# FFN phases of a transformer trunk: 512-wide matmul passes split into 256-wide ones behind a few wide passes

## The reference

```python
D_MODEL = 1024
SEQ = 256
D_FF = ((8 * D_MODEL // 3 + 127) // 128) * 128
...
def _swiglu(h, w_gate, w_up, w_down):
    return (jax.nn.silu(h @ w_gate) * (h @ w_up)) @ w_down
...
for i in range(DEPTH):
    x = x + 0.5 * _swiglu(_rms_norm(x, norm_ffn1[i]), ffn1_w_gate[i], ffn1_w_up[i], ffn1_w_down[i])
    h = _rms_norm(x, norm_mix[i])
    ...
    x = x + y
    x = x + 0.5 * _swiglu(_rms_norm(x, norm_ffn2[i]), ffn2_w_gate[i], ffn2_w_up[i], ffn2_w_down[i])
```

## Time and profile before

| | |
|---|---|
| median of three runs | 1985.58 us (1983.98 to 1986.40) |
| the profiled execution's own time | 1984.08 us |
| its span, first to last instruction | 1982.3 us |
| TensorE busy, matmuls | 1951.4 us, 98% |
| VectorE busy | 1421.3 us, 72% |
| ScalarE busy | 1044.6 us, 53% |
| mean granted TensorE clock | 0.997 |
| DMA | 350.14 MB, 177 GB/s |

### The profile page before, as it was taken

How to read it: one execution, slowest core, us unless ns; L and a number is a source line. 1 busy time by engine, 2 the same in 40 slices (tenths; PEclk the granted TensorE clock), 3 DMA queues, 4 the chain that set the end, 5 groups by cost and what they waited for, 6 DMA issues and landing times.

```text
span 1982.3 us, 29082 instructions
## 1 busy us (share of the span) xinstructions
PE 1951.4 (98%) x12574; PEld 1717.7 (87%) x12574; DVE 1421.3 (72%) x1645; ACT 1044.6 (53%) x1250; POOL 102.3 (5%) x114
## 2 busy tenths in 40 slices
PE   7999999999999998999999999999999999999999
PEld 6888889888888896988888898788888888888887
DVE  7776678875787555877587658887758765778763
ACT  6554566554555344654465455575446544566542
POOL 3000001000200002100100000010000000001000
PEclk9999999999999999999999999999999999999999
DMA  7655434655665683665666553356565655435653
GB/s 237 193 184 182 149 128 150 192 187 192 194 192 181 201 246 88 190 191 187 195 191 192 184 178 127 109 180 191 182 197 188 193 185 179 142 128 171 191 189 108
DMA packets 336365, 350.14 MB, mean 177 GB/s; under 512 B 10077, under 2 KB 331886, under 8 KB 336238
## 3 DMA queue, kind: packets, MB, share of 16 engines
q1 hardware_dynamic: 331742, 343.58, 54.4%
q10 hardware_dynamic: 4496, 4.70, 1.2%
HBM read 346.04 MB, written 2.22 MB: 176 GB/s over the span
## 4 chain that ended last, share of the span: by engine, by line
PE 92%; DVE 3%; ACT 2%; DMA 1%; issue 1%; POOL 1%; ACTq 0%; SPq 0%; DVEq 0%; POOLq 0%
PE banks L1443 48%; PE banks L1448 25%; PE banks L1434 5%; PE banks L1436 4%; PE banks L1435 4%; PE banks L1660 1%; PE banks L1713 1%; DMA u_away<-sb_u_pad 1%; ACT sb_w_high L470 1%; DVE sb_w_low L808 1%; PE banks L1680 1%; PE banks L1697 1%; PE banks L1901 1%; ACT sb_scores L598 0%; PE banks L1818 0%
## 5 line engine op out<-in xcount | busy, mean ns | idle before, releaser
L808 DVE TENSOR_TENSOR sb_w_low<-sb_raw,sb_w_high 128x2048 fp32r<-128x2048 f32 (+1 forms) x332 | 750.2, 2263 | 211.3 <-ACT sb_w_high L470 210.7
L1443 PE MATMUL banks<-sb_x_both,sb_w_high 128*128 128x512 f32 x2816 | 720.7, 393 | 2.3 <-ACT sb_w_high L470 2.3
L470 ACT ACTIVATE sb_w_high<-sb_raw 128x2048 fp32r<-128x2048 f32 (+1 forms) x332 | 618.9, 1869 | 123.9 <-DMA sb_raw<-in_ffn_w_down 108.2
L1443 PEld LDWEIGHTS banks<-sb_x_both,sb_w_high 128*128 128x128 f32 x2816 | 498.5, 188 | 82.8 <-ACT sb_w_high L470 2.5
L1448 PEld LDWEIGHTS banks<-sb_x_both,sb_w_low 128*128 128x128 f32 x2792 | 386.1, 188 | 35.4
L1448 PE MATMUL banks<-sb_x_both,sb_w_low 128*128 128x256 f32 x2792 | 394.1, 278 | 0.0
L1443 PE MATMUL banks<-sb_h_both,sb_w_high 128*128 128x512 f32 x1408 | 355.5, 392 | 0.0
L1443 PEld LDWEIGHTS banks<-sb_h_both,sb_w_high 128*128 128x128 f32 x1408 | 250.7, 188 | 43.0
L1448 PEld LDWEIGHTS banks<-sb_h_both,sb_w_low 128*128 128x128 f32 x1408 | 190.9, 188 | 15.4
L1448 PE MATMUL banks<-sb_h_both,sb_w_low 128*128 128x256 f32 x1408 | 195.4, 279 | 0.0
L488 ACT ACTIVATE sb_x_both<-sb_xT,sb_vec 128x256 fp32r<-128x256 f32 x96 | 43.3, 500 | 197.6 <-DVE sb_xT L841 173.1
(11 more groups left out here) (229 smaller groups left out, 1932.5 us busy)
## 6 DMA issues: line engine op xcount, KB each, us to landing
sb_raw<-in_ffn_w_gate SPq DMA_DIRECT2D x88, 1024.0 KB, 5.3
sb_raw<-in_ffn_w_up SPq DMA_DIRECT2D x88, 1024.0 KB, 5.4
sb_raw<-in_ffn_w_down SPq DMA_DIRECT2D x64, 1024.0 KB, 5.0
sb_raw<-in_ffn_w_down SPq DMA_DIRECT2D x32, 768.0 KB, 4.3
sb_raw<-in_fox_w_in SPq DMA_DIRECT2D x24, 1024.0 KB, 5.3
sb_raw<-in_conv_w_pw SPq DMA_DIRECT2D x12, 1024.0 KB, 5.5
sb_raw<-in_diff_w_in SPq DMA_DIRECT2D x12, 1024.0 KB, 5.1
sb_raw<-in_fox_w_out SPq DMA_DIRECT2D x8, 1024.0 KB, 5.0
```

The costliest lines, as they stand in the source:

```text
L470: act.activation(slot(w_high, b)[:, 0:width(b)], slot(raw, b)[:, 0:width(b)], ACT.Copy).then_inc(S["high_ready"], 1)
L808: dve.tensor_tensor(slot(w_low, b)[:, 0:width(b)], slot(raw, b)[:, 0:width(b)], slot(w_high, b)[:, 0:width(b)].bitcast(F32), ALU.subtract) ...
L1443: return pe.matmul(pair(bank[at][:, :]), high[:, n * P:(n + 1) * P], m_both, start=first, stop=last, skip_group_check=True)
```

## The change

The phases' second pair and everything behind it use a new helper, `few_wide`, in place of `both_parts`. Of a tile's k it does the first `wide` ones with a wide pass each; the others with two narrow passes, one for each half of the bank (`on_part`), on the same weights; then the low passes for all k. The first pair keeps its order. `wide` is 0 (`WIDE`) but for these: in the first phase the four tiles of the second pair have 4, 5, 3 and 3, and the two tiles of the down block behind `turn_vectors` 3 and 4; in the other seven phases the first tile of the second pair has 4.

```diff
@@ -33,6 +33,7 @@
 WINDOW = SEQ + SHIFTS * (ROUNDS - 1)
 PADDED = WINDOW + SHIFTS - 1
 RING = 5
+WIDE = 0
 FF_TILES = D_FF // P
 DOWN = [(0, 8), (8, 16), (16, FF_TILES)]
 MASKED = -1e30
@@ -1459,6 +1460,25 @@
                     ins = on_both(at, n, high[:, k, :], m_both(k), False, last and k == ks[-1])
                 return ins
 
+            def on_part(at, n, high, m_part, half, first, last):
+
+                return pe.matmul(bank[at][:, half * SEQ:(half + 1) * SEQ], high[:, n * P:(n + 1) * P], m_part,
+                                 start=first, stop=last, skip_group_check=True)
+
+            def few_wide(at, n, high, low, m_both, ks, first, last, wide):
+
+                for k in ks[:wide]:
+                    on_both(at, n, high[:, k, :], m_both(k), first and k == ks[0], False)
+                for k in ks[wide:]:
+                    for half in range(2):
+                        on_part(at, n, high[:, k, :], m_both(k)[:, half, :], half,
+                                first and k == ks[0] and half == 0, False)
+                for k in ks[:-1]:
+                    on_high(at, n, low[:, k, :], m_both(k)[:, 0, :])
+                k = ks[-1]
+                return pe.matmul(bank[at][:, SEQ:2 * SEQ], low[:, k, n * P:(n + 1) * P], m_both(k)[:, 0, :],
+                                 start=False, stop=last, skip_group_check=True)
+
             def columns_half(dst, b, n, tiles=range(KT)):
 
                 high, low = (slot(t, b).rearrange("p (k n) -> p k n", k=KT) for t in (w_high, w_low))
@@ -1551,9 +1571,12 @@
             def ffn(i):
                 b, f = starts[i], number(i)
 
-                def tile(which, p, n, ks):
+                def tile(which, p, n, ks, wide=None):
                     blk = b + 2 * p + which
                     high, low = (slot(t, blk).rearrange("p (k n) -> p k n", k=KT) for t in (w_high, w_low))
+                    if wide is not None:
+                        return few_wide(pair_banks(p) + 2 * which + n, n, high, low, lambda k: x_both[:, :, k, :],
+                                        list(ks), ks[0] == 0, ks[-1] == KT - 1, wide)
                     return both_parts(pair_banks(p) + 2 * which + n, n, high, low, lambda k: x_both[:, :, k, :],
                                       list(ks), ks[0] == 0, ks[-1] == KT - 1)
 
@@ -1593,6 +1616,18 @@
                             if T == 3:
                                 ins.then_inc(S["block_done"], 1)
 
+                def wide_of_tile(p, which, n):
+                    if p > 1:
+                        return WIDE
+                    if i == 0:
+                        return (4, 5, 3, 3)[2 * which + n]
+                    return 4 if which == 0 and n == 0 else WIDE
+
+                def wide_of_chunk(T, c, n):
+                    if i == 0 and T == 1 and c == 1:
+                        return 3 + n
+                    return WIDE
+
                 def one_pair(p):
                     pe.wait_ge(S["hidden_ready"], PAIRS * f + p - 1)
                     for which in range(2):
@@ -1600,7 +1635,7 @@
                         for n in range(2):
                             if p == 1 and which and n:
                                 pe.wait_ge(S["root_ready"], i + 1)
-                            ins = tile(which, p, n, range(KT))
+                            ins = tile(which, p, n, range(KT), wide_of_tile(p, which, n))
                         ins.then_inc(S["block_done"], 1)
 
                 def down(T, c):
@@ -1614,8 +1649,9 @@
                     high, low = (slot(t, blk)[:, 0:width(blk)].rearrange("p (k n) -> p k n", n=256)
                                  for t in (w_high, w_low))
                     for n in range(2):
-                        ins = both_parts(2 * (T % 2) + n, n, high, low, lambda k: h_both[:, :, first + k, :],
-                                         list(range(last - first)), c == 0, c == len(DOWN) - 1)
+                        ins = few_wide(2 * (T % 2) + n, n, high, low, lambda k: h_both[:, :, first + k, :],
+                                       list(range(last - first)), c == 0, c == len(DOWN) - 1,
+                                       wide_of_chunk(T, c, n))
                     ins.then_inc(S["block_done"], 1)
 
                 if i:
```

## The result

| | before | after |
|---|---|---|
| median, 16 runs each | 1985.57 us (1983.0 to 1987.86) | 1992.78 us (1987.03 to 2005.54) |
| the profiled execution's own time | 1984.08 us | 1991.08 us |
| its span | 1982.3 us | 1989.3 us |

The ratio, taken over all runs, is 1.0047, with a 95% interval of 1.0033 to 1.0061 (the two medians alone give 1.0036): slower by about half a per cent, where 1967 was forecast, and 0.8 us outside the range. The runs also spread over 18.5 us, against 4.9 before.

The account below looks back on a forecast made before the run. TensorE, busy for 98% of the span, was taken as the bound; narrow passes at the low price in all eight FFN phases gave -18.8 us, less 1.5 us lost at the last phase's end: 1967 us, range 1962 to 1992.

Parts of the forecast that it names:

- The prices and the sums per phase: FFN phases: a narrow pass costs 113.4 or 117.8 ns, one price per phase; 168.8 or 175.3 us a phase.
- Entry of the phases behind a mixer: Four FFN phases: three more wide passes end in a 394 with a 388 due, so low price.
- Entry of the phases behind an FFN phase: Three FFN phases: first wide pass's position uncertain; low price given a little over half.
- Rival 1: The three phases after an FFN phase lock at the high price: 19.5 us back, 1986.3; chance 0.18.
- Counting three ways: Entry after an FFN phase: three possible sequences of wide passes, two ending at the low price, one at the high.
- Entry of the first phase: First FFN phase: wide passes 4, 5, 3, 3 in four tiles give the low price from the third tile on.
- The end of the last phase: Last down projection, behind the output's transposes: 116 triples at the high price lose 1.5 us of the gain.
- The sum: Whole kernel: -18.8 + 1.5 = -17.3 us on 1984.1, giving 1966.8, predicted as 1967.
- between the phases: Everything outside the FFN phases, fox included: no change, costed at nothing.
- The rule that spoke against the change: Every matmul: fixed cost of about 2.5 ns, so 3,918 splits cost 9.8 us, giving 1994.

Follow-up runs that it names:

- runs 10 and 11: The changed kernel run twice more with no edit; single profiled executions of 2007.29 and 2006.03 us.
- experiment 1: Against the changed kernel, phases 3, 5 and 7 open with five wide passes in place of four; 1973.72 us, ratio to before 0.9943.
- experiment 2: Against the changed kernel, phases 2, 4, 6 and 8 open with five wide passes in place of four; 2001.98 us, ratio to before 1.0099.
- experiment 6: Against the changed kernel, three wide passes added at the head of the sixth pair in phases 3, 5 and 7; 1981.00 us, ratio to before 0.9963.
- experiment 5: Against the changed kernel, three more wide passes head the second pair's second tile in phases 2 to 8; 1970.62 us, ratio to before 0.9914.
- chain of seven: Against the changed kernel, seven wide passes mixed with narrow ones over two tiles replace the few wide passes in all phases; 1968.73 us, ratio to before 0.9902.

## Why the prediction was wrong

**The prices and the sums per phase: right.** The predicted 168.8 and 175.3 us came out as 168.7 and 175.3. The low price was 113.3 (taken: 113.4), the high one 117.8, and in no phase did one change into the other without a wide pass, transposes or a stall. 3,918 splits were made, VectorE's and ScalarE's busy times moved by under 1 us, and TensorE got no gap (busy for all 175.00 us of the window 523:698).

**Entry of the phases behind a mixer: right in this execution**, all four at the low price at once, by the count of positions. That this entry is not fixed for phases 4 and 6 the prediction did not see: it took one profiled execution's positions as the program's, and that all four came out as counted was in part luck: in runs 10 and 11 phases 4 and 6 did not. Before, the next wide run came after eight narrow passes and a wrong position mended itself, so its runs lay within 4.9 us and gave no warning; with narrow passes alone a position lasts 1,480 passes and the runs spread over 18.5.

**Entry of the phases behind an FFN phase: the step that failed.** The prediction had "by the narrow passes alone the first wide pass acted like a 392 ... high price", and then gave the low price a little over half, because the pass's own length was hidden. Rival 1 came true: three phases at 175.3, 19.7 us. The three passes behind the first were 393, 398, 394, not 394, 388, 392, so it was no 392 either; it is a position of its own, one wide pass short of the place with a 388 due, and a fifth wide pass would have set the low price (experiment 1). Counting three ways and weighing them evenly was the error: two of them started from positions that the earlier trace rows show behind other passes, and the one count that came from this very phase said high. The sign that the two entries differ could be read too. Single lines of the kernel before, the last two wide passes ahead of the sum of squares and the first behind it, in phase 2 and in phase 3:

```profile
L1443 PE MATMUL banks<-sb_x_both,sb_w_high x3: 392/399/587, 338.5 to 339.2; 128*128 128x512 f32 x3
```

```profile
L1443 PE MATMUL banks<-sb_x_both,sb_w_high x3: 388/393/585, 521.2 to 521.9; 128*128 128x512 f32 x3
```

587 behind a 399 and 585 behind a 393: to 0.01 us, as in the earlier trace rows, these are 0.59 and 0.58, one step of the last digit, and the prediction stopped there.

**Entry of the first phase: failed as well**, 176.9 us where 172.7 - 2.28 = 170.4 had been worked out, a further 6.5. The count 4, 5, 3 led to the low price where the first wide pass took the 419 ns of the kernel before to the next start and the clock stayed up (experiments 1, 2 and 6, 170.6 us). But the phase begins behind a wait of some 2.5 us for GpSimd, and its first position is not fixed: in experiment 5 the first pass took 420, the wide passes behind it were 398, 394, 394, and the five of the next tile ended in 392, the high price, 175.4. In the kernel after it took 416, then came 388, 392, 394, and again five that ended in 392. After had, in addition, a stretch at the lower clock. Windows of the kernel after and then of the kernel before (us; busy time and count of PE, PEld, DVE, ACT, POOL; granted clock; DMA share; GB/s):

```profile
13.00:17.00 4.00, 4.00 (x15) 3.28 (x16) 4.00 (x6) 4.00 (x7) 0.84 (x1) 1.00 1.10 348
29.50:33.50 4.00, 4.00 (x21) 3.87 (x19) 3.93 (x4) 3.97 (x4) 0.45 (x1) 0.57 0.60 204
```

```profile
13.00:17.00 4.00, 4.00 (x15) 3.31 (x15) 4.00 (x6) 4.00 (x7) 0.83 (x1) 0.57 1.10 348
29.50:33.50 4.00, 4.00 (x25) 3.52 (x24) 3.93 (x4) 3.97 (x5) 0.40 (x1) 1.00 0.60 197
```

Before, the granted clock lay mostly at the lower level (1.2 GHz) at 13 to 17 us, while blocks were still arriving at 348 GB/s; after, at 29.5 to 33.5, behind the wait and the four wide passes, which still ran at full clock: it is the 16 narrow passes of the first tile that went slowly. Of 6.5 us the lower clock is an estimated 1.6 (176.9 against 175.4 in experiment 5), the position the rest. In the kernel after the count was off before the stretch began. In the third execution (run 11) it was not: the first pass took 419 and the next two 226 and 233, as in experiment 1, then the clock fell, the five wide passes behind the stretch ended in 392, where experiment 1 had 388, and the phase took 176.96. So across such a stretch a right count was lost as well. Single lines of the four wide passes in the kernel after, and of those five in the third execution (their order is 393, 388, 397, 397, 392):

```profile
L1444 PE MATMUL banks<-sb_x_both,sb_w_high x4: 388/393/579, 28.5 to 29.4; 128*128 128x512 f32 x4
```

```profile
L1444 PE MATMUL banks<-sb_x_both,sb_w_high x5: 388/393/397, 33.9 to 34.8; 128*128 128x512 f32 x5
```

**The end of the last phase: right.** 344 narrow passes behind the transposes ran at the high price (348 counted), 1.5 us; the chain of seven there brought 171.6 to 170.6.

**The sum.** 1966.8 + 19.7 (phases 3, 5, 7) + 6.5 (phase 1) - 1.8 (between the phases, mostly fox, which had been costed at nothing) = 1991.2; the profiled execution took 1991.1. The median of 16 runs, 1992.8, is probably a mixture of such executions: each further phase behind a mixer that falls to the 585 entry adds 6.6.

**The rule that spoke against the change.** The estimate from the Trainium skill, "TensorE: Matmul & The Clock Gate", section "Wait — 56ns, not 53.3ns?", was 1994, and the median is 1992.8; but by the phases the two agree by accident. A fixed cost for each matmul can make no phase of 168.7 us beside one of 175.3 with equal counts, and with 3,884 splits the chain of seven is 1% faster than before.

## What to carry to other kernels

Before an edit takes away the passes that set a condition, ask how long the condition then lasts and whether the start is the same in every execution: what was mended every few passes becomes a matter of one entry. Make the entry insensitive (a chain that ends in the wanted position from each position that occurs) rather than count it out from one profile, and look at several profiles of the same program. Two durations that differ by 2 ns, 585 and 587, were here the difference of 6.6 us a phase; where a summary rounds them to its last digit, read the single lines.

## What the runs showed of the hardware that was not expected

The price of a 256-column pass in fp32r is one of two, 113.3 or 117.8 ns from start to start at the full clock, and stays through 1,480 passes on changing weights and banks; inside the FFN phases of the 13 traces it changes only behind wide passes or an interruption (transposes, a stall). The position that sets it is not wiped out by the float32 matmul of the sum of squares (91 entries of 91). The low price was met behind wide passes only where they ended in 394 with a 388 due. That can be read off the lengths: in all 13 traces every run of six or more narrow passes right behind wide ones at full clock was at the low price where the last two of them were 392, 394 or 394, 394, and at the high price behind any other ending (398, 394 among them). From the high price three wide passes led there where they were 397, 394, 394 (experiments 5 and 6). No run here shows which part of the chip holds this position; the three distances of wide passes, 226, 229 and 232 ns, suggest something with a period of three passes, and that is only an inference.
